# Banded attention as a stage of its own: six heads of prefetch, begun in the projection, outputs and one bias table kept in SBUF, stores from GpSimd's queue

## What is computed

```python
def dilated_band_attention(q, k, v, pos, bias_table, window, dilation):
    ...
    s = jnp.einsum('bgnqhc,bgnkhc->bgnhqk', qb, kb).astype(jnp.float32) * (Dh ** -0.5)
    rel = pkb[:, :, :, None, :] - pqb[..., None]
    bias = bias_table[t5_bucket(rel)]
    s = s + jnp.moveaxis(bias, -1, 3).astype(jnp.float32)
    ...
    m = jnp.max(s, axis=-1, keepdims=True)
    p = jnp.exp(s - m)
    den = jnp.sum(p, axis=-1, keepdims=True)
    o = jnp.einsum('bgnhqk,bgnkhc->bgnqhc', (p / den).astype(v.dtype), vb)
    lse = (m + jnp.log(den))[..., 0]
...
        wts = jax.nn.softmax(jnp.stack(lses), axis=0)
        o_b = jnp.einsum('gbsh,gbshc->bshc', wts.astype(x.dtype), jnp.stack(outs)).reshape(B, S, D)
        g_a, g_b = jnp.split(jax.nn.sigmoid(gates), 2, axis=-1)
        x = x + gt1 * ((g_a * o_a + g_b * o_b) @ w_out[l])
```

## Time and profile before

| | us |
|---|---|
| median of 3 runs | 3958.83 |
| lowest, highest | 3957.23, 3964.39 |
| profiled execution | 3959.2 |
| its span in the trace | 3957.5 |

### The profile page before, as it was taken

One profiled execution on the slowest core, in us unless ns is written; L12 is line 12 of the kernel. 1 busy time (PEld: TensorE's weight loads), 2 busy tenths in 40 slices (PEclk: granted clock), 3 DMA queues, 4 the chain that ended last, 5 costly groups with the idle time before them and its releaser, 6 DMA issues. The chain is left out here.

```text
span 3957.5 us, 42882 instructions
## 1 busy us (share of the span) xinstructions
PE 3272.2 (83%) x16212; PEld 1627.2 (41%) x16212; DVE 1346.4 (34%) x3105; ACT 679.5 (17%) x1388; POOL 310.9 (8%) x401
## 2 busy tenths in 40 slices
PE   6779599849975999099999975649369999999998
PEld 4445344324543444054444445315144344443444
DVE  6414211142432111599994024223432121222212
ACT  1124122122211221200000023213111011010111
POOL 1113011130011111200000000000010000000000
PEclk9889699969986999599999987769679999999999
DMA  6851699631016996343323375341639999999995
GB/s 231 257 193 60 234 367 351 237 102 45 1 54 220 362 359 243 113 167 119 125 98 127 105 229 182 113 139 46 259 144 395 407 406 423 407 407 406 406 422 213
DMA packets 307376, 907.96 MB, mean 229 GB/s; under 512 B 37168, under 2 KB 96832, under 8 KB 257088
## 3 DMA queue, kind: packets, MB, share of 16 engines
q1 hardware_dynamic: 280048, 821.60, 55.9%
q0 software_dynamic: 27216, 84.88, 5.7%
HBM read 816.57 MB, written 89.81 MB: 229 GB/s over the span
## 5 line engine op out<-in xcount | busy, mean ns | idle before, releaser
L2838 PE MATMUL ec_gu<-ec_ring,ec_xg 128*64 128x512 f32 x2048 | 454.6, 595 | 0.9 <-ACT ec_xg L2990 0.9
L205 PE MATMUL proj_ps<-xT,proj_w 128*128 128x512 f32 x992 | 434.4, 601 | 16.0 <-DMA proj_w<-in_na_w_in 16.0
L2489 DVE SCALAR_TENSOR_TENSOR proj_acc<-proj_hit,proj_row,proj_acc 128x128 f32<-128x128 f32 (+2 forms) x768 | 416.0, 613 | 7.2
L205 PE MATMUL proj_ps<-proj_w,xT 128*128 128x512 f32 (+2 forms) x896 | 356.6, 561 | 14.7 <-DMA proj_w<-in_w_in 14.7
L205 PEld LDWEIGHTS proj_ps<-xT,proj_w 128*128 128x128 f32 x992 | 190.7, 193 | 256.7 <-issue 239.5
L2838 PEld LDWEIGHTS ec_gu<-ec_ring,ec_xg 128*64 128x64 f32 x2048 | 142.0, 137 | 303.3 <-issue 303.3
L205 PEld LDWEIGHTS proj_ps<-proj_w,xT 128*128 128x128 f32 x896 | 171.1, 191 | 198.7 <-issue 154.3
L2867 PE MATMUL ec_yp<-ec_ring,ec_hT 128*64 128x512 f32 x1024 | 248.5, 636 | 0.0
L1410 PE MATMUL moe_gu_ps<-moe_w,moe_xg 128*64 128x512 f32 x1024 | 232.6, 608 | 17.8 <-ACT moe_xg L1525 17.8
L976 PE MATMUL mix_o<-mix_w,xT 128*128 128x512 f32 x384 | 173.8, 614 | 19.4 <-DMA mix_w<-in_w_out 19.4
L229 ACT ACTIVATE proj_o<-proj_ps 128x512 f32<-128x512 f32 (+2 forms) x104 | 60.2, 579 | 633.0 <-PE proj_ps L205 632.1
(11 more groups left out here) (492 smaller groups left out, 3736.9 us busy)
## 6 DMA issues: line engine op xcount, KB each, us to landing
ec_ring<-in_w_gate SPq DMA_DIRECT2D x128, 1024.0 KB, 8.8
ec_ring<-in_w_up SPq DMA_DIRECT2D x128, 1024.0 KB, 10.9
ec_ring<-in_w_down SPq DMA_DIRECT2D x128, 1024.0 KB, 12.4
moe_w<-in_exp_w_gate SPq DMA_DIRECT2D x32, 2048.0 KB
moe_w<-in_exp_w_up SPq DMA_DIRECT2D x32, 2048.0 KB
moe_w<-in_exp_w_down SPq DMA_DIRECT2D x32, 2048.0 KB, 11.6
proj_w<-in_w_in SPq DMA_DIRECT2D x22, 2048.0 KB
proj_w<-in_w_ada SPq DMA_DIRECT2D x16, 1536.0 KB
```

Of the source, the lines that this page charges most:

```text
L205: mm = nc.tensor.matmul(bank[0:jb["op"], 0:jb["ow"]], lhs, rhs, start=(k == 0), stop=(k == nk - 1))
L2489: V.scalar_tensor_tensor(acc[:, h, 0:wd], self.hit[r][:, 0:wd], self.row[r][:, h:h + 1], acc[:, h, 0:wd], ALU.mult, ALU.add)
L2838: mm = nc.tensor.matmul(gu_ps[n][half, :], xg[:, k, c0:c0 + CAP], w[:, m * D_FF + n * 512:m * D_FF + (n + 1) * 512], start=(k == 0), stop= ...
```

## The change

- The projection's jobs come in another order: latents, band 0's queries, keys and values, gates, then bands 1 and 2. `gemms` gets the argument `ahead`: after the side work's `finish`, SyncE waits until the first eight chunks are stored and issues the first loads of the banded attention (`BandBuffers.first`).
- Their buffers are allocated before the projection. Four of band 0's seven value tiles lie in `h`, a tile of the block that is free at that time.
- Band 1's bias table stays in the SBUF tile in which VectorE builds it; its store and its 8 loads are gone. The fill of band 0's table is cut from 4 DMAs to 16, and the tile that it reads shrinks by four.
- The banded attention is a function of its own, with the same loop on TensorE, VectorE and ScalarE. Six heads of queries and keys and four of bias are in flight. SyncE only loads. Outputs go into SBUF tiles that hold all heads: `xT` for band 0, `h` for band 1, the value tile of band 1 for band 2. GpSimd stores bands 1 and 2 in halves of four heads (rows of 2 KB), and the statistics of all three. Maximum and sum are written straight into the statistics, without the two copies.
- The stage is followed by a second clearing of semaphores and a second barrier, for the prefetch's semaphores.
- `merge` reads band 0's output from SBUF.

The rows below are the order of instructions on one engine, with row number, line, operation and tile.

The two copies are gone; the rest stands in the same order. The diff, cut to what matters:

```diff
-def gemms(nc, name, jobs, side=None, clear=(), order=None, slots=2, after=None):
+def gemms(nc, name, jobs, side=None, clear=(), order=None, slots=2, after=None, ahead=None):
...
+                if ahead:
+                    kept = range(saved.index(ahead[0]) + 1)
+                    for r in range(2):
+                        sp.wait_ge(stored[r], 16 * len(kept[r::2]))
+                    ahead[1](sp)
...
-FILL = UNIT0 * 4 * DIL_H // P // 4
+FILLS = 16
+FILL = UNIT0 * 4 * DIL_H // P // FILLS
...
-        self.acc = {g: st.sb(f"acc{g}", [P, DIL_H, BIAS_WIDTH[g]]) for g in groups}
+        self.acc = {g: self.kept[g] if g in self.kept else st.sb(f"acc{g}", [P, DIL_H, BIAS_WIDTH[g]]) for g in groups}
...
-            q.wait_ge(self.ready, n + 1)
-            done += self.store(q, g)
+            if g not in self.kept:
+                q.wait_ge(self.ready, n + 1)
+                done += self.store(q, g)
...
+    R, RB = 6, 4
...
+    def load_qk(self, sp, n):
+        g, h, r = n // DIL_H, n % DIL_H, n % self.R
+        sp.dma_start(self.q[r][:], self.qks[g][h * P:(h + 1) * P, :]).then_inc(self.qk_in[r], 16)
+        sp.dma_start(self.k[r][:], self.qks[g][D + h * P:D + (h + 1) * P, :]).then_inc(self.qk_in[r], 16)
...
+    def first(self, sp):
+        self.load_qk(sp, 0)
+        self.load_bias(sp, 0)
+        self.load_v(sp, 0)
+        self.load_qk(sp, 1)
+        self.load_bias(sp, 1)
+        self.load_qk(sp, 2)
+        self.load_qk(sp, 3)
...
+    og = [xT[:].rearrange("p (u a) s -> p u (a s)", u=U), h[:], bb.v1[:]]
...
+            @block.sync
+            def _(sp):
+                bb.load_bias(sp, 2)
+                bb.load_bias(sp, 3)
+                bb.load_qk(sp, 4)
+                bb.load_qk(sp, 5)
+                bb.load_v(sp, 1)
+                for n, (g, h_) in enumerate(heads):
+                    if n + R < len(heads):
+                        sp.wait_ge(s_ready, last_of[n] + 1)
+                        bb.load_qk(sp, n + R)
+                    if g != 1 and (h_ < RB or g == 0):
+                        sp.wait_ge(max_ready, last_of[n] + 1)
+                        bb.load_bias(sp, h_ + RB + (H if g == 2 else 0))
+                    if n == 2:
+                        bb.load_v(sp, 2)
...
+            @block.gpsimd
+            def _(pool):
+                sent = 0
+                for n, (g, h_) in enumerate(heads):
+                    if h_ % 4 == 3 and g:
+                        pool.wait_ge(out_done, last_of[n] + 1)
+                        cut = slice((h_ - 3) * P, (h_ + 1) * P)
+                        for u in range(U):
+                            to = dilated_views(g)[1](ogs[g], u)
+                            pool.dma_start(to[:, :, cut] if g == 2 else to[:, cut], og[g][:, u, cut]).then_inc(stored, 16)
+                            sent += 1
+                    if h_ == H - 1:
+                        pool.wait_ge(out_done, last_of[n] + 1)
+                        for u in range(U):
+                            pool.dma_start(dilated_views(g)[1](sts[g], u), stat[g][:, u, :, :].rearrange("p h s -> p (h s)")) \
+                                .then_inc(stored, 16)
+                            sent += 1
+                pool.wait_ge(stored, 16 * sent)
...
+                    V.scalar_tensor_tensor(ssb[s % 3][:], s_ps[s % 3][:], P ** -0.5, bias, ALU.mult, ALU.add)
+                    V.drain()
+                    V.tensor_reduce(stat[g][:, us[0]:us[-1] + 1, h_, 0], ssb[s % 3][:].rearrange("p (b n) -> p b n", n=nk),
+                                    AX.X, ALU.max, negate=True).then_inc(max_ready, 1)
...
+                    dve.wait_ge(exp_done, s + 1)
+                    if g:
+                        V.tensor_reduce(dn, pr[s % 4][:].rearrange("p (b n) -> p b n", n=nk), AX.X, ALU.add)
+                        V.drain()
+                    V.reciprocal(rd, dn)
+                    V.drain()
+                    dve.wait_ge(pv_done, s + 1)
+                    V.tensor_tensor(og[g][:, us[0]:us[-1] + 1, h_ * P:(h_ + 1) * P],
+                                    o_ps[s % 2][:, 0:B * P].rearrange("p (b d) -> p b d", d=P),
+                                    rd.unsqueeze(2).to_broadcast([P, B, P]), ALU.mult).then_inc(out_done, 1)
...
-                    for n, src in enumerate([oa] + ogs):
+                    for n, src in ((0, oa), (2, ogs[1]), (3, ogs[2])):
...
-                    dve.wait_ge(ld[t], 16 * 5)
+                    dve.wait_ge(ld[t], 16 * 4)
...
-        gemms(nc, "proj2", [job(win, 0, 2, n_lat // 2, xT, P, S, lat, "N"),
-                            job(win, n_lat + 9 * D, 4, 512, xT, P, S, gates, "N")]
-              + [job(win, at[g], 4, 512, xT, P, S, qks[g], "T", tok=dilated_views(g)[0]) for g in range(3)]
-              + [job(win, at[g] + 2 * D, 2, 512, xT, P, S, vs[g], "N") for g in range(3)],
-              side=lambda st: RelativeBias(nc, a, biases, (0, 1), st))
...
+        with ExitStack() as c1:
+            acc1 = c1.enter_context(nc.sbuf_tensor("bias_acc1", [P, DIL_H, BIAS_WIDTH[1]], F32))
+            bb = BandBuffers(nc, c1, qks, vs, biases, h, acc1)
+            qk_jobs = [job(win, at[g], 4, 512, xT, P, S, qks[g], "T", tok=dilated_views(g)[0]) for g in range(3)]
+            v_jobs = [job(win, at[g] + 2 * D, 2, 512, xT, P, S, vs[g], "N") for g in range(3)]
+            gemms(nc, "proj2", [job(win, 0, 2, n_lat // 2, xT, P, S, lat, "N"), qk_jobs[0], v_jobs[0],
+                                job(win, n_lat + 9 * D, 4, 512, xT, P, S, gates, "N"),
+                                qk_jobs[1], v_jobs[1], qk_jobs[2], v_jobs[2]],
+                  side=lambda st: RelativeBias(nc, a, biases, (0, 1), st, {1: acc1}), ahead=(7, bb.first))
+            bb.rest()
+            band_attention(nc, ident, bb, xT, h, ogs, sts)
+            nc.clear_and_free_semaphores(bb.sems)
+            nc.all_engine_barrier()
```

206 lines of the change are left out of this document (168 added, 38 removed).

## The result

The changed kernel takes **3907.01 us** (median of 4 runs, 3902.47 to 3913.55) where the kernel before, run beside it, takes 3960.32 us (3957.23 to 3964.39). The ratio is 0.9866, 95% interval 0.9849 to 0.9883. It is 53 us faster, where 75 were forecast, and 3 us above the range given.

A forecast was written before the change was run, and what follows sets the result against it. The prediction took the banded attention to be bound by late transfers, loads standing behind an earlier head's stores, not by bandwidth. 71.6 + 1.5 + 1.6 = 74.7 us off the profiled 3959.2 gave 3884.5, predicted median 3884, range 3876 to 3904.

The forecast's parts named there:

- Part 1: Projection: first attention loads land by 2320 us, so the third group of scores begins at 2339.3, not 2351.90.
- the rival of a late prefetch: Before the attention: prefetch held behind the bias stores, 12.6 us lost at the start, 3897 us; chance 0.05.
- The turns: Banded attention loop: 2.285 us a turn in band 0 on TensorE, 2.97 in bands 1 and 2 on VectorE.
- Part 2: Banded attention: loads behind no store remove 72 us of key waits; last output at 2423.1 against 2494.69, 71.6 us earlier.
- The cover of part 2: Band 0: 10.5 MB at 335 GB/s land 31 us in, before head 7's bias is wanted 33 us in.
- a rival of 5 us: Band 0 bound by bandwidth: at 280 GB/s head 7's bias comes 5 us late, 3889 to 3894; chance 0.13.
- Part 3: Attention's end: GpSimd stores, band 0's output kept in SBUF; tail 9.4 us against 10.9, 1.5 gained, ends +4 to -4.
- the landing: Attention's end, after the last issue: 4.6 us until stores land and the stage ends, plus 0.5 for the second barrier.
- Part 4: Merge: three outputs loaded instead of four, 0.524 MB fewer at 335 GB/s, 1.6 us off VectorE's first wait.
- GpSimd's queue: Rival in the attention's stores: 28 issues become the bound; at 3.3 us each, 3928 us in total; chance 0.03.
- The 3.1 us weighed in part 3: Skill's figure for a GpSimd transfer beside a copy: 87 us of queue if all 28 were hit, kernel some 3923 us.
- The granted clock: Rival in bands 1 and 2: TensorE's clock falls, turns take 4.43 us; 3903, or 3893.5 if every second; chance 0.09.

The follow-up runs named there:

- e12: Changed kernel with the banded attention's first loads issued at that stage's start instead of within the projection: ratio 0.9907 to the kernel before.
- e3: Kernel before with only band 2's four value loads cut into 16 of 32 rows: ratio 0.9957 to the kernel before.
- e8: Kernel before with only the banded attention's outputs and statistics stored by GpSimd's queue instead of SyncE's: 3931.00 us.
- e9: Kernel before with banded attention's outputs and statistics stored by GpSimd's queue and band 2's value loads cut into 16 of 32 rows: 3919.24 us.
- e1: Changed kernel with band 2's four value loads cut into 16 of 32 rows, at the same place: ratio 0.9837 to the kernel before.
- e4: e1 with band 2's outputs and statistics stored as 128 contiguous rows a unit, leaving results in another row order: ratio 0.9818 to the kernel before.
- e16: Changed kernel, band 2's value loads in 16 pieces at heads 8 to 11, its stores contiguous, merge reading token order: ratio 0.9822 to the kernel before.

## Why the prediction was right, and where it failed

**Part 1, prefetch: right.** The tables were stored in 13.12 us, the loads issued from 2300.55, the scores ran at the stage's start, and the rival of a late prefetch did not come true. It is worth 17.0 us (e12).

**The turns: right.** The part up to the last output was forecast at 2423.1 - 2335.5 = 87.6 us, and is 85.9 once nothing waits. Bands 1 and 2 turn in 2.97 us as worked out; band 0 in 2.20 instead of 2.285, which included a wait.

**Part 2, loads that no longer wait: this is the step that failed.** It said that the loads were late because they stood behind stores "and not because bandwidth is short". That held for 29 us. Most of the longest wait, 21.2 us, belonged to the four value loads: cutting them took 13.4 us off it in e3 and 15.4 us off it where GpSimd stored (e8 to e9). The change keeps them: it moved them from band 1 into band 0, where they cost 19.2 us of bias wait. In the prediction's own sum for band 0 they are 2.1 of the 10.5 MB at 335 GB/s; they went at 102. Term of the sum: 105.2 instead of 87.6 us. They stood in the trace of before:

```profile
2391.72 1.74 SPq L525 DMA_DIRECT2D og<-dil_o  x4
...
2396.82 5.59 SPq L504 DMA_DIRECT2D dil_v<-dv  x4
2402.46 7.56 SPq L525 DMA_DIRECT2D og<-dil_o  x4
```

```profile
2402.00:2406.00 4.00, 1.03 (x7) 0.84 (x6) 1.91 (x6) 1.60 (x5) 0.00 (x0) 0.93 0.26 105
2406.00:2412.00 6.00, 0.00 (x0) 0.00 (x0) 0.00 (x0) 0.00 (x0) 0.00 (x0) 0.50 0.38 137
```

Four issues that take 5.59 us, stores behind them of 7.56 where the same stores took 1.74 a head earlier, and a DMA share of 0.26 and then 0.38 while the engines run dry and stand. I took the mean 0.47 of rows 1 as a sign of spare capacity; it was an average over stretches with full engines and stretches like these.

**The cover of part 2, capacity in band 0** was named with a margin of 1 us and a rival of 5 us. It seems real: 5.7 us are left in e1 after the narrow loads are cut, with full engines. That it is near the rival's 5 us is luck, since in e1 the 32-row pieces carry 245 GB/s and not the rival's 280, and behind a larger cause it is only what is left.

**Part 3, the tail: mis-sized.** Issues were priced at 0.53 and took 0.53 to 0.70 us. The term that fell was the landing: 4.6 us, "since these stores are far smaller than the projection's". Together the four are 1 MB, as much as the projection's last store. At a full rate that would have gone out within the issues, as it does in e4 and e16, and there the 4.6 + 0.5 us after the last issue are met with 5.08. But the stretch of the tail carries 139 GB/s, and bytes move until 5 us after the last issue. 15.7 instead of 9.4 us, so a loss of 4.8 against before, just beyond the worst end given (-4).

**Part 4, merge: mis-sized.** From the merge's first load to VectorE's first product were 2788.42 - 2771.49 = 16.93 us and are 2741.80 - 2725.11 = 16.69: 0.2 us instead of 1.6. VectorE's wait fell from 6.14 to 5.40 us, but the twelve loads of statistics ahead of it took 6.78 us to issue instead of 6.25. So 0.7 us came off the wait, not 1.6, and most of it was lost in the issues; why one load fewer gave only 0.7 was not tested.

**The other rivals.** GpSimd's queue stayed cheap, also beside VectorE's long rows: 2.80 us for four, 0.70 each. The 3.1 us weighed in part 3 were no test of this change: the Trainium skill's "SBUF — State Buffer", section "Who interferes with whom", names copies among what locks GpSimd out and says that `tensor_reduce` does not, and here VectorE ran no copy beside GpSimd's issues; the 0.70 us agree. The granted clock fell to 0.50 within the long wait (the table by stretch above), was back at 1.00 by 2395, and stayed there through the rest of bands 1 and 2 with gaps in every turn:

```profile
2400.00:2420.00 20.00, 18.25 (x154) 17.09 (x153) 18.45 (x35) 12.22 (x35) 2.81 (x6) 1.00 0.78 260
2420.00:2441.00 21.00, 15.22 (x119) 13.36 (x117) 19.13 (x36) 11.14 (x31) 7.06 (x12) 1.00 0.38 99
```

The account: 17.6 us up to the last output and 6.3 in the tail are the 23.9 us by which the stage, at 120.9, exceeds the forecast 97.0; the merge adds 1.4. That makes 25.3 of the 29 us between the forecast 3884.5 and the profiled 3913.55. The other 3.7 lie outside these stages, 1.6 of them ahead of the attention, and are less than what executions differ by.

## What to carry to other kernels

When a queue of transfers is late, look at the DMA share within the wait itself and not at its mean. Here 0.26 to 0.29 stood for transfers on some 4 of 16 engines. They held up whatever was issued behind them, at both places at which they were tried; cutting them helped, and spreading the pieces over a stretch with room took the rest. A long issue in the SyncE rows (11 us for four where others take 2) marks them before anything is changed. And price a layout on both sides: here contiguous stores took 6.4 us off one stage and put 7.7 on the stage that reads them back.
